# A trunk layer in float32 pieces: who splits the second output tile's weights, and when two late modulation steps run

## The chip, the cores and the metric

The kernel runs on one core of a Trainium2 chip. The metric is the time of one execution on the device in microseconds, taken as the median of several runs. The core has five engines with queues of their own: TensorE (PE, matrix products), VectorE (DVE), ScalarE (ACT), GpSimd (POOL) and SyncE (SP, which here issues all DMAs). They wait for each other through semaphores, counters that one engine raises and another waits on.

## The reference, cut to what matters

One layer of a diffusion backbone on 1024 tokens of width 1024, with a context of 256 tokens. The change lies around the output projection and the residual behind it, the last lines here:

```python
sh1, sc1, g1, sh2, sc2, g2 = [m[:, None, :] for m in adaln(c, w_mod[l], b_mod[l], N_MOD)]
h = modulate(x, norm1_w[l], sh1, sc1)
proj = h @ w_in[l]
...
# mix_and_mlp
mix = jnp.concatenate([y_gla, y_conv, y_pool], axis=-1) @ w_out
x = x + g1 * mix
h2 = modulate(x, norm2_w, sh2, sc2)
return x + g2 * (jnp.square(jax.nn.relu(h2 @ w_mlp1)) @ w_mlp2)
```

`adaln` is SiLU(c) times a 1024 x 6144 matrix; its six parts of 1024 columns are the shifts, scales and gates. The final RMSNorm follows. All in float32.

## The kernel before, in words

**Stages.** Tiles 0 to 19 of the weight stream are the input projection (`PROJ`), tiles 20 to 27 (`T_OUT` = 20, called output tiles 0 to 7 here) the output projection, then the first two tiles of the MLP, then the MLP with its own scheme of seven products in place of eight. In the input projection a tile is split by ScalarE (`weight_high`, L1411) and VectorE (`weight_low`, L1947). From output tile 0 on GpSimd does both passes (`split`, L766 and L769): a multiplication by ones for the high part, a subtraction for the low part.

**Around the change.** When the last input tile (CB1) is done, ScalarE rounds the six mixed blocks that were not ready earlier and VectorE subtracts (`low_mix(2)` to `low_mix(7)`); TensorE's output tile 0 takes the blocks in the same order and waits for each (`lo_made`). GpSimd, in queue order, splits output tile 0, output tile 1 (when CB1 is done and its slot so free), output tile 2 (when output tile 0 is done), and so on: `split_pairs`. TensorE waits at the start of each tile for `split_done`.

**The residual.** VectorE adds each finished output tile, times the gate, to `X` (`add`, L2189, which reads PSUM and frees one of TensorE's two accumulators), ScalarE squares the result and scales it (L1619, L1621), and VectorE adds the squares to `acc2` (L2192).

**Late modulation.** Two of the six parts of `adaln` (`sh2`, `g2`) are summed here by VectorE in 16 steps (`add_late(0)` to `add_late(15)`, L2173): a 128 x 1024 block of the matrix times a scalar, added to one of two sums. All operands lie in SBUF. The blocks, 512 KB each, come through four buffers: `load_late(i)` (L629) waits for step i - 4 from i = 4 on (`late_taken`). Before the change steps 0 to 3 stand ahead of the first addition to the residual, and two steps behind each of the six whole additions. TensorE needs the sums (`modulations_late`) in the last pair of output tiles.

**SP's queue** runs strictly in order: once all low parts are made (`lo_made`, 8) it issues `load_late(0)` to `(3)`, the second half of `X` (2 MB, L634), `load_late(4)` to `(7)`, then `load_tile(23)`, the weights of output tile 3; then for each further tile two late loads and the tile:

```python
sp.wait_ge(lo_made, KT)
for i in range(4):
    load_late(i)
sp.dma_start(X[:, 4:8, :], xt[4:8].rearrange("k p n -> p k n")).then_inc(x2_loaded[1], 16)
for i in range(4, 8):
    load_late(i)
load_tile(T_OUT + 3)
```

The order on each engine is the order in which the code is written; there is no planner in this part.

Of the kernel before, what the change touches and what calls it, by code (L numbers as in the profile page):

```python
# [19 lines left out]
ACT = mybir.ActivationFunctionType  # L20
# [32 lines left out]
T_OUT = NPROJ  # L53
# [146 lines left out]
def hybrid_trunk(nc, wstream, wg_in, wm1, wm2, xt, ct, small_in, gw_in, out):  # L200
    ctx = ExitStack()
    with ctx:
# [13 lines left out]
        raw = at("raw", [P, 2, KT, P], F32, raw_at)  # L216
        w_hi = at("w_hi", [P, 2, KT, P], F32R, w_hi_at)
# [156 lines left out]
        raw_loaded = [sem("raw_loaded0"), sem("raw_loaded1")]  # L374
# [6 lines left out]
        hi_made = sem("hi_made")  # L381
        split_done = sem("split_done")
        tile_done = sem("tile_done")
# [118 lines left out]
        def stream_free(t):  # L502

            return M_OF[PROJ[t]] + 1 if t < NPROJ else M_OUT + t - NPROJ + 1
# [248 lines left out]
        def _(pool):  # L753
# [10 lines left out]
            def split(b, n, linked):  # L764

                pool.tensor_tensor(w_hi[:, b, :, :], raw[:, b, :, :], ones.unsqueeze(1).broadcast_to([P, KT, P]),  # L766
                                   ALU.mult).then_inc(linked, 1)
                pool.wait_ge(linked, n)
                pool.tensor_tensor(w_lo[:, b, :, :], raw[:, b, :, :], w_hi[:, b, :, :].bitcast(F32),  # L769
                                   ALU.subtract).then_inc(split_done, 1)  # L770
# [17 lines left out]
            for t in range(NPROJ):  # L788
# [11 lines left out]
                if t >= 2 and PROJ[t - 2] in ("P0", "P1"):  # L800

                    i = int(PROJ[t - 2][1])
# [16 lines left out]
                        backward_states(h)  # L819
                        pool.wait_ge(states_backward, (NCH - 1) * (h + 1))  # L820
            pool.wait_ge(split_done, T_OUT)
            for t in (T_OUT, T_OUT + 1):
                pool.wait_ge(raw_loaded[t % 2], 16 * (t // 2 + 1))
                pool.wait_ge(tile_done, stream_free(t - 2))
                split(t % 2, t + 1, hi_made)
            def split_pairs(first, last):
                with pool.Fori(first, last) as i:
                    for b in range(2):
# [542 lines left out]
        def _(act):  # L1371
# [210 lines left out]
            for t, name in enumerate(PROJ):  # L1582
# [8 lines left out]
                m, i = M_OF[name], int(name[-1])  # L1591
# [9 lines left out]
            for n, k in enumerate(MIX_ORDER):  # L1601
# [8 lines left out]
                src, shape = mix_block(k)  # L1610
                act.activation(shape(mix_parts(k)[0]), src, ACT.Copy).then_inc(mix_hi, 1)  # L1611

            def residual_squares(m0, acc_made, sq_made, nth, sums_done, rs_made, between, after):

                def square(i, b):
                    act.wait_ge(main_free[1 - b], i + ((m0 + b) // 2 + 1))
                    act.wait_ge(acc_made, i * 2 + (b + 1))
                    xk = X[:, bass.ds(i * 2 + b, 1), :]
                    act.activation(sq2[:, :].unsqueeze(1), xk, ACT.Square).then_inc(sq_made, 1)  # L1619
                    if nth == 0:  # L1620
                        act.activation(xg[:, :, bass.ds(i * 2 + b, 1), :],  # L1621
                                       X[:, bass.ds(i * 2 + b, 1), :].rearrange("p k (h c) -> p h k c", h=2), ACT.Copy,
                                       scale=gain2[:, bass.ds(i * 2 + b, 1)]).then_inc(xg_made, 1)

                with act.Fori(0, KT // 2 - 1) as i:
                    for b in range(2):
                        square(i, b)

                def square_half(k, half, s_out):
                    cols = slice(half * HALF, (half + 1) * HALF)  # L1630
                    act.activation(sq2[:, cols], X[:, k, cols], ACT.Square).then_inc(s_out, 1)

                def scale_half(k, half):
                    if nth == 0:
                        cols = slice(half * HALF, (half + 1) * HALF)
                        act.activation(xg[:, half, k, :], X[:, k, cols], ACT.Copy, scale=gain2[:, k:k + 1]).then_inc(xg_made, 1)

                act.wait_ge(acc_made, KT - 1)
                act.wait_ge(res_half, 2 * nth + 1)
                square_half(KT - 2, 0, sq_made)  # L1640
                scale_half(KT - 2, 0)
                act.wait_ge(acc_made, KT)
                act.wait_ge(res_half, 2 * nth + 2)
                square_half(KT - 1, 0, sq_last)
                scale_half(KT - 1, 0)
                act.wait_ge(sums_done, 1)
                rsqrt(rs2[:, 0:HALF], sm[:, 0, :], D, rs_made)
                act.wait_ge(main_free[1], (m0 + KT - 2) // 2 + 1)
                square_half(KT - 2, 1, sq_made)
                scale_half(KT - 2, 1)  # L1650
                between()
                act.wait_ge(acc_made, KT + 1)
                act.wait_ge(main_free[0], (m0 + KT - 1) // 2 + 1)
                square_half(KT - 1, 1, sq_last)
                after()
                scale_half(KT - 1, 1)
                act.wait_ge(sums_done, 2)
                rsqrt(rs2[:, HALF:N], sm[:, 1, :], D, rs_made)
# [224 lines left out]
        def _(dve):  # L1883
# [61 lines left out]
            def weight_low(t):  # L1945
                dve.wait_ge(hi_made, t + 1)
                tt(w_lo[:, t % 2, :, :], raw[:, t % 2, :, :], w_hi[:, t % 2, :, :].bitcast(F32),  # L1947
                   ALU.subtract).then_inc(split_done, 1)
# [184 lines left out]
            def low_mix(n):  # L2133

                dve.wait_ge(mix_hi, n + 1)
                src, shape = mix_block(MIX_ORDER[n])
                hi, lo = mix_parts(MIX_ORDER[n])
                tt(shape(lo), src, shape(hi.bitcast(F32)), ALU.subtract).then_inc(lo_made, 1)  # L2138
# [3 lines left out]
            for t, name in enumerate(PROJ):  # L2142
# [8 lines left out]
                m, i = M_OF[name], int(name[-1])  # L2151
# [10 lines left out]

            for n in range(2, KT):
                low_mix(n)

            def add_late(i):

                dve.wait_ge(late_loaded[i % 4], 16 * (i // 4 + 1))
                if i < 2:
                    dve.wait_ge(late_cleared, 1)  # L2170
                else:
                    dve.wait_ge(late_taken, i - 1)
                stt(out=macc_late[:, i % 2, :], in0=mbuf_late[:, i % 4, :], scalar=silu_c[:, 2 * (i // 2):2 * (i // 2) + 1],  # L2173
                    in1=macc_late[:, i % 2, :], op0=ALU.mult, op1=ALU.add).then_inc(late_taken, 1)

            dve.wait_ge(o_done, 2 * HEADS)
            dve.memset(macc_late[:, :, :], 0.0).then_inc(late_cleared, 1)
            for i in range(4):
                add_late(i)

            def residual(m0, g, acc_made, sq_made, nth, between, after):

                dve.memset(acc2[:, :], 0.0).then_inc(acc_made, 1)
                dve.wait_ge(acc_made, 1)

                def add(i, b):
                    dve.wait_ge(tile_done, i * 2 + (m0 + b + 1))
                    xk = X[:, bass.ds(i * 2 + b, 1), :]
                    stt(out=xk, in0=main[:, 1 - b:2 - b, :], scalar=mods[:, g, bass.ds(i * 2 + b, 1)], in1=xk,  # L2189
                        op0=ALU.mult, op1=ALU.add).then_inc(main_free[1 - b], 1)  # L2190
                    dve.wait_ge(sq_made, i * 2 + (b + 1))
                    tt(acc2[:, :], acc2[:, :], sq2[:, :], ALU.add).then_inc(acc_made, 1)  # L2192
                    dve.wait_ge(acc_made, i * 2 + (b + 2))

                for i in range(KT // 2 - 1):
                    if i == 2:
                        dve.wait_ge(x2_loaded[1], 16)
                    for b in range(2):
                        add(i, b)
                        for n in range(2):  # L2200
                            add_late(4 + 4 * i + 2 * b + n)

                def add_half(k, half, s_out):
                    cols = slice(half * HALF, (half + 1) * HALF)
                    stt(out=X[:, k, cols], in0=main[:, (k + 1) % 2, cols], scalar=mods[:, g, k:k + 1], in1=X[:, k, cols],
                        op0=ALU.mult, op1=ALU.add).then_inc(s_out, 1)

                def sum_half(half):
                    cols = slice(half * HALF, (half + 1) * HALF)
                    dve.wait_ge(sq_made, KT - 1 + half)  # L2210
                    tt(acc2[:, cols], acc2[:, cols], sq2[:, cols], ALU.add).then_inc(acc_made, 1)

                dve.wait_ge(half_done, 2 * nth + 1)
                add_half(KT - 2, 0, res_half)
                sum_half(0)
                dve.wait_ge(half_done, 2 * nth + 2)
                add_half(KT - 1, 0, res_half)
                between()
                dve.wait_ge(tile_done, m0 + KT - 1)
                add_half(KT - 2, 1, main_free[1])  # L2220
                sum_half(1)
                after()
                dve.wait_ge(tile_done, m0 + KT)
                add_half(KT - 1, 1, main_free[0])
# [365 lines left out]
```

## Time and profile before

| what | value |
|---|---|
| median of 3 runs | 1144.76 us (1144.01 to 1144.79) |
| profiled execution | 1144.1 us |
| its span | 1142.3 us |
| TensorE matmul busy | 1093.3 us, 96% |
| VectorE busy | 833.2 us, 73% |
| ScalarE busy | 507.9 us, 44% |
| GpSimd busy | 336.1 us, 29% |
| mean granted clock of TensorE | 0.988 |

The profile records one execution. Times in it count from the start of its span, in microseconds; `L924` is a line of the kernel. A busy share is an average over stages with different limits. In a timeline, "[0.72 <-DVE X L2189]" behind an instruction says that its engine sat idle for 0.72 us before it, and that the last thing to arrive was VectorE's write of X at line 2189.

### The profile page before, as it was taken

How to read it: one execution, taken by the hardware profiler on the slowest of the kernel's cores; microseconds unless marked ns; L12 is line 12 of the kernel's file. 1: busy time of each engine (PE TensorE's matmuls, PEld its weight loads, DVE VectorE, ACT ScalarE, POOL GpSimd, SP SyncE). 2: the span in 40 equal slices, each digit the busy share in tenths (PEclk: the TensorE clock that was granted, in tenths of full speed). 3: DMA queues.
4: the chain of work that ended last, by engine and by line, in shares of the span. 5: the costliest groups of instructions: out<-in, count | busy, mean ns of one | idle time of the engine just before them, and what ended most of it. 6: DMA issues, size and time to landing. Idle time of an engine off the chain costs nothing.

```text
span 1142.3 us, 15381 instructions
## 1 busy us (share of the span) xinstructions
PE 1093.3 (96%) x5056; PEld 866.1 (76%) x5056; DVE 833.2 (73%) x1068; ACT 507.9 (44%) x823; POOL 336.1 (29%) x295
## 2 busy tenths in 40 slices
PE   8889999999999899887999999999899999999995
PEld 4468888877888688566888888888687877787783
DVE  3777869636444875799777777777977777687776
ACT  4556523355624222347666666666422122122234
POOL 1000006386202353522323233333322132123233
PEclk9899999999999999899999999999999999999998
DMA  9423241001013673204865757677827745955703
GB/s 370 195 93 100 88 144 38 25 32 38 20 37 129 239 237 132 74 9 155 329 263 225 267 222 264 222 270 272 336 96 273 278 186 198 331 211 187 263 1 147
DMA packets 58894, 199.71 MB, mean 175 GB/s; under 512 B 5600, under 2 KB 6880, under 8 KB 58336
## 3 DMA queue, kind: packets, MB, share of 16 engines
q1 hardware_dynamic: 58848, 199.11, 47.3%
q8 instruction: 28, 0.46, 0.2%
q14 instruction: 18, 0.15, 0.0%
HBM read 139.32 MB, written 59.77 MB: 174 GB/s over the span
## 4 chain that ended last, share of the span: by engine, by line
PE 45%; DMA 3%; DVE 2%; issue 1%; ACT 1%; SPq 0%; POOL 0%; DVEq 0%
PE main L1341 13%; PE ob L1300 13%; PE sm L1300 10%; PE sm L1341 5%; PE ob L1341 3%; DMA raw<-wstream 3%; DVE XR L2435 1%; DVE stage_last L2332 0%; SPq L662 0%; POOL XR L907 0%; DVE stage L2332 0%; DVE XR L2495 0%; ACT slot L1704 0%; DVE t_tmp L2325 0%; DVE hid L2345 0%
## 5 line engine op out<-in xcount | busy, mean ns | idle before, releaser
L1300 PE MATMUL ob<-h_sum,slot 128*128 128x512 f32 x540 | 133.3, 396 | 5.0 <-ACT hid L1747 3.1
L1704 ACT ACTIVATE slot<-raw 128x512 fp32r<-128x512 f32 x80 | 50.4, 631 | 181.0 <-PE main L1341 71.5
L924 PE MATMUL main<-a_hi,w_hi 128*128 128x512 f32 x376 | 125.9, 416 | 2.6 <-DVE a_lo L2138 2.6
L1300 PEld LDWEIGHTS ob<-h_sum,slot 128*128 128x128 f32 x540 | 102.3, 190 | 29.5 <-issue 3.9
L924 PE MATMUL main<-a_lo,w_hi 128*128 128x512 f32 x376 | 116.7, 392 | 0.0
L924 PE MATMUL main<-a_hi,w_lo 128*128 128x512 f32 x376 | 116.2, 390 | 0.0
L2435 DVE SCALAR_TENSOR_TENSOR XR<-main,mods,XR 128x512 f32<-128x512 f32 x112 | 82.8, 747 | 30.8 <-PE main L1341 29.1
L924 PEld LDWEIGHTS main<-a_hi,w_hi 128*128 128x128 f32 x376 | 66.7, 188 | 21.1 <-issue 5.8
L924 PEld LDWEIGHTS main<-a_hi,w_lo 128*128 128x128 f32 x376 | 70.6, 188 | 15.7
L924 PEld LDWEIGHTS main<-a_lo,w_hi 128*128 128x128 f32 x376 | 70.6, 188 | 15.6
L1300 PE MATMUL sm<-h_hi,slot 128*128 128x512 f32 x240 | 79.7, 393 | 0.6 <-ACT hid L1747 0.6
L2280 DVE TENSOR_TENSOR slot<-raw,slot 128x512 fp32r<-128x512 f32 x75 | 64.1, 855 | 21.7 <-ACT slot L1692 21.7
L1341 PE MATMUL main<-t_even,slot 128*128 128x512 f32 x336 | 79.3, 393 | 0.0
L782 POOL TENSOR_TENSOR scaled_state<-tst,decay 64x128 f32<-64x128 f32 x60 | 28.0, 467 | 162.6 <-ACT tst L1482 158.0
L1341 PEld LDWEIGHTS main<-t_even,slot 128*128 128x128 f32 x336 | 63.1, 188 | 14.2
L2285 DVE TENSOR_TENSOR slot<-raw,slot 128x512 fp32r<-128x512 f32 x80 | 57.6, 737 | 20.4 <-ACT slot L1704 20.4
L881 POOL TENSOR_TENSOR part_sum<-raw 128x512 f32<-128x512 f32 x16 | 21.3, 1333 | 137.8 <-DMA raw<-wstream 109.9
L766 POOL TENSOR_TENSOR w_hi<-raw,small 128x1024 fp32r<-128x1024 f32 x10 | 25.1, 2513 | 111.2 <-PE main L924 99.5
L865 POOL TENSOR_TENSOR held<-raw 128x512 f32<-128x512 f32 x15 | 24.9, 1657 | 111.5 <-DVE slot L2280 111.5
L1300 PEld LDWEIGHTS sm<-h_hi,slot 128*128 128x128 f32 x240 | 45.1, 188 | 11.0 <-issue 1.0
L1341 PE MATMUL main<-stage,slot 128*128 128x512 f32 x168 | 48.5, 397 | 3.6 <-DVE stage_last L2332 3.6
L2435 DVE SCALAR_TENSOR_TENSOR XR<-sm,mods,XR 128x512 f32<-128x512 f32 x64 | 46.5, 743 | 5.8 <-PE sm L1341 5.1
(334 smaller groups left out, 2508.7 us busy)
## 6 DMA issues: line engine op xcount, KB each, us to landing
hidden_kept<-stage SPq DMA_DIRECT2D x98, 512.0 KB, 4.3
raw<-wstream SPq DMA_DIRECT2D x60, 512.0 KB, 4.0
t_even<-hidden_kept SPq DMA_DIRECT2D x56, 512.0 KB, 4.6
raw<-wstream SPq DMA_DIRECT2D x16, 1024.0 KB, 7.9
stage<-hidden_kept SPq DMA_DIRECT2D x21, 512.0 KB, 3.7
stage_last<-hidden_kept SPq DMA_DIRECT2D x21, 512.0 KB, 4.6
wmod<-wm SPq DMA_DIRECT2D x4, 2048.0 KB, 23.4
mbuf<-wm SPq DMA_DIRECT2D x16, 512.0 KB, 3.9
```

What stands on the lines that cost most here:

```text
L766: pool.tensor_tensor(w_hi[:, b, :, :], raw[:, b, :, :], ones.unsqueeze(1).broadcast_to([P, KT, P]), ALU.mult).then_inc(linked, 1)
L782: pool.tensor_tensor(scaled_state[DK:P, :], tst[DK:P, h % 2, c, :], decay[DK:P, h, c:c + 1].broadcast_to([DK, DV]), ALU.mult).then_inc(sta ...
L865: pool.tensor_tensor(sums, a12, a11, ALU.subtract).then_inc(w1_sum, 1)
L881: pool.tensor_tensor(sums, a21, a22, ALU.add).then_inc(w2_sum, 1)
L924: ins = pe.matmul(main[:, bank, half * HALF:(half + 1) * HALF], w[:, slot, k, :], x[:, half * HALF:(half + 1) * HALF], start=begin, stop=end)
L1300: ins = pe.matmul(hid_bank(acc, odd), slots1[j][:, w, kp, :], parts[x][:, kp, :], start=PARTS[j][3] and kp == 0 and m == 0, stop=kp == KP ...
L1341: ins = pe.matmul(product_bank(s, acc, q), slots2[j][:, w, q, kp, :], tset[odd][j][kp][:, x, :], start=begins and kp == 0 and n == 0, stop ...
L1704: act.activation(slots2[j][:, 0, :, :, :], operand(s, j), ACT.Copy).then_inc(w2_hi, 1)
L2280: tt(slots1[j][:, 1, :, :], operand1(b, j), slots1[j][:, 0, :, :].bitcast(F32), ALU.subtract).then_inc(w1_lo, 1)
L2285: tt(slots2[j][:, 1, :, :, :], operand(s, j), slots2[j][:, 0, :, :, :].bitcast(F32), ALU.subtract).then_inc(w2_lo, 1)
L2435: stt(out=XR[m][:, cols], in0=product_bank(s, acc, q), scalar=mods[:, 3, m:m + 1], in1=XR[m][:, cols], op0=ALU.mult, op1=ALU.add).then_inc ...
```

## The change

Output tile 1's weights (stream tile `T_OUT + 1`) are no longer split by GpSimd: ScalarE writes the high part behind its last mix copy, VectorE the low part behind `low_mix(7)`. GpSimd waits for that split's end and goes on with the pairs from output tile 2. Late modulation steps 2 and 3 move from ahead of the first addition to the residual to behind it, so that four steps (2 to 5) follow that addition; the order of the steps among themselves, and the positions of steps 4 to 15, stay. SP's and TensorE's programs are unchanged.

```diff
--- before.py
+++ after.py
@@ -819,10 +819,10 @@
                         backward_states(h)
                         pool.wait_ge(states_backward, (NCH - 1) * (h + 1))
             pool.wait_ge(split_done, T_OUT)
-            for t in (T_OUT, T_OUT + 1):
-                pool.wait_ge(raw_loaded[t % 2], 16 * (t // 2 + 1))
-                pool.wait_ge(tile_done, stream_free(t - 2))
-                split(t % 2, t + 1, hi_made)
+            pool.wait_ge(raw_loaded[T_OUT % 2], 16 * (T_OUT // 2 + 1))
+            pool.wait_ge(tile_done, stream_free(T_OUT - 2))
+            split(T_OUT % 2, T_OUT + 1, hi_made)
+            pool.wait_ge(split_done, T_OUT + 2)
             def split_pairs(first, last):
                 with pool.Fori(first, last) as i:
                     for b in range(2):
@@ -1610,6 +1610,12 @@
                 src, shape = mix_block(k)
                 act.activation(shape(mix_parts(k)[0]), src, ACT.Copy).then_inc(mix_hi, 1)
 
+
+            act.wait_ge(split_done, T_OUT + 1)
+            act.wait_ge(raw_loaded[(T_OUT + 1) % 2], 16 * ((T_OUT + 1) // 2 + 1))
+            act.wait_ge(tile_done, stream_free(T_OUT - 1))
+            act.activation(w_hi[:, (T_OUT + 1) % 2, :, :], raw[:, (T_OUT + 1) % 2, :, :], ACT.Copy).then_inc(hi_made, 1)
+
             def residual_squares(m0, acc_made, sq_made, nth, sums_done, rs_made, between, after):
 
                 def square(i, b):
@@ -2162,6 +2168,7 @@
 
             for n in range(2, KT):
                 low_mix(n)
+            weight_low(T_OUT + 1)
 
             def add_late(i):
 
@@ -2175,8 +2182,8 @@
 
             dve.wait_ge(o_done, 2 * HEADS)
             dve.memset(macc_late[:, :, :], 0.0).then_inc(late_cleared, 1)
-            for i in range(4):
-                add_late(i)
+            add_late(0)
+            add_late(1)
 
             def residual(m0, g, acc_made, sq_made, nth, between, after):
 
@@ -2197,8 +2204,9 @@
                         dve.wait_ge(x2_loaded[1], 16)
                     for b in range(2):
                         add(i, b)
-                        for n in range(2):
-                            add_late(4 + 4 * i + 2 * b + n)
+                        at = 4 * i + 2 * b + (2 if (i, b) == (0, 0) else 4)
+                        for n in range(at, 8 + 4 * i + 2 * b - 2):
+                            add_late(n)
 
                 def add_half(k, half, s_out):
                     cols = slice(half * HALF, (half + 1) * HALF)
```

## Rows read from the trace of the kernel before

**Rows 1.** TensorE's timeline (start us, length us): starts of output tiles 0 to 4.
```profile
369.71 0.63 PE L924 MATMUL main<-early_hi,w_hi 128*128 128x512 f32 x2
...
376.90 0.74 PE L924 MATMUL main<-a_hi,w_hi 128*128 128x512 f32 x2 [1.67 <-DVE a_lo L2138]
...
383.88 0.63 PE L924 MATMUL main<-early_hi,w_hi 128*128 128x512 f32 x2
...
395.77 0.73 PE L924 MATMUL main<-early_hi,w_hi 128*128 128x512 f32 x2 [0.72 <-DVE X L2189]
...
406.88 0.40 PE L924 MATMUL main<-early_hi,w_hi 128*128 128x512 f32 x1
...
417.89 0.63 PE L924 MATMUL main<-early_hi,w_hi 128*128 128x512 f32 x2
```

**Rows 2.** Timeline of GpSimd (POOL): splits of output tiles 1 to 4.
```profile
370.02 2.41 POOL L766 TENSOR_TENSOR w_hi<-raw,small 128x1024 fp32r<-128x1024 f32 x1 [5.96 <-PE main L924]
...
372.51 3.26 POOL L769 TENSOR_TENSOR w_lo<-raw,w_hi 128x1024 fp32r<-128x1024 f32 x1
...
384.12 2.40 POOL L766 TENSOR_TENSOR w_hi<-raw,small 128x1024 fp32r<-128x1024 f32 x1 [8.36 <-PE main L924]
...
400.57 2.47 POOL L766 TENSOR_TENSOR w_hi<-raw,small 128x1024 fp32r<-128x1024 f32 x1 [10.72 <-DMA raw<-wstream]
...
403.12 2.40 POOL L769 TENSOR_TENSOR w_lo<-raw,w_hi 128x1024 fp32r<-128x1024 f32 x1
...
407.12 3.06 POOL L766 TENSOR_TENSOR w_hi<-raw,small 128x1024 fp32r<-128x1024 f32 x1 [1.60 <-PE main L924]
```

**Rows 3.** Timeline of VectorE (DVE): low parts, late steps, first addition and its sum.
```profile
371.05 2.46 DVE L2138 TENSOR_TENSOR a_lo<-ypool,a_hi 128x1024 fp32r<-128x1024 f32 x1
...
373.44 3.41 DVE L2138 TENSOR_TENSOR a_lo<-ypool,a_hi 128x1024 fp32r<-128x1024 f32 x1
...
376.77 1.21 DVE L2138 TENSOR_TENSOR a_lo<-yconv,a_hi 128x1024 fp32r<-128x1024 f32 x1
...
381.76 1.76 DVE L2177 MEMSET macc_late<- 128x2048 f32 x1 [0.38 <-issue]
...
384.69 2.90 DVE L2173 SCALAR_TENSOR_TENSOR macc_late<-mbuf_late,silu_c,macc_late 128x1024 f32<-128x1024 f32 x1 [1.16 <-DMA mbuf_late<-wm]
...
387.52 3.41 DVE L2173 SCALAR_TENSOR_TENSOR macc_late<-mbuf_late,silu_c,macc_late 128x1024 f32<-128x1024 f32 x1
...
393.49 0.91 DVE L2183 MEMSET acc<- 128x1024 f32 x1 [0.16 <-issue]
...
394.43 1.28 DVE L2189 SCALAR_TENSOR_TENSOR X<-main,mods,X 128x1024 f32<-128x1024 f32 x1
...
397.02 1.23 DVE L2192 TENSOR_TENSOR acc<-acc,sq 128x1024 f32<-128x1024 f32 x1 [1.31 <-ACT sq L1619]
...
398.28 2.48 DVE L2173 SCALAR_TENSOR_TENSOR macc_late<-mbuf_late,silu_c,macc_late 128x1024 f32<-128x1024 f32 x2
```

**Rows 4.** ScalarE's and VectorE's timeline: an earlier split; end of ScalarE's pause.
```profile
351.36 1.04 ACT L1411 ACTIVATE w_hi<-raw 128x1024 fp32r<-128x1024 f32 x1
...
352.44 1.23 DVE L1947 TENSOR_TENSOR w_lo<-raw,w_hi 128x1024 fp32r<-128x1024 f32 x1 [9.26 <-ACT w_hi L1411]
...
395.93 1.06 ACT L1619 ACTIVATE sq<-X 128x1024 f32 x1 [20.22 <-DVE X L2189]
```

**Rows 5.** SP: issue of tile 3's weights; landings of weights issued at 401.2, 411.7.
```profile
393.72 0.43 SPq L595 DMA_DIRECT2D raw<-wstream  x1
...
DMA to landing us min/median/max: 5.2/5.2/5.2
...
DMA to landing us min/median/max: 4.3/4.3/4.3
```

**Rows 6.** TensorE behind a stall: timeline, windows (granted clock third from last).
```profile
472.58 0.62 PE L1265 MATMUL main<-h_hi,w_hi 128*128 128x512 f32 x1 [3.44 <-DVE h_lo L2241]
...
476.00:478.00 2.00, 2.00 (x5) 1.48 (x6) 2.00 (x4) 0.00 (x0) 0.00 (x0) 0.50 0.00 0
```

## The prediction

> **What bounds the kernel now.** The matrix engine is busy nearly throughout, so a change beside it is worth only what it takes off a wait of that engine, and only if the next wait does not give it back. I read its timeline over the first output tiles first [rows 1]. A clean output tile takes 11.01 us (406.88 to 417.89). Tile 0 takes 383.88 - 369.71 = 14.17 us, 3.16 too many, and the row at 376.90 names who ended one of its two stalls: VectorE's low parts of the mixed activations (L2138). Tile 1 takes 395.77 - 383.88 = 11.89, 0.88 too many, ended by VectorE's first addition to the residual (L2189). Tile 2 takes 11.11: its first pair of matmuls after a stall is some 0.1 slow. So 3.16 + 0.88 + 0.10 = 4.14 us is all that this stage can return; tiles 3 to 5 run without a gap.
>
> Then GpSimd's and VectorE's timelines, side by side [rows 2, 3]. A low part takes 1.21 us with nothing on GpSimd (376.77) and one follows the other 1.14 later. The two at 371.05 and 373.44 take 2.46 and 3.41. The first ends at 373.51, 1.08 after GpSimd's split instruction of 370.02 (ended 372.43); the second ends at 376.85, 1.08 after the one of 372.51 (ended 375.77, 3.26 long for the usual 2.41; 2.26 of it behind VectorE's end at 373.51). So GpSimd and a VectorE instruction with both inputs in SBUF take turns: whoever started second waits for the whole of the other. An addition that reads PSUM doesn't wait (394.43: 1.28).
>
> **Part 1: the split of output tile 1's weights leaves GpSimd.** GpSimd's two instructions (2.41 + 3.26) go. ScalarE gets one copy, 1.04 us (at 351.36) [rows 4], right behind its last mix copy near 375.7: it has nothing else until 395.93, an idle time of 20.22, so it costs nothing there. VectorE gets one subtraction, 1.23 (at 352.44) [rows 4], behind the six low parts. These now run unblocked: six by 1.14 from 371.05 end at 377.94, where before they ended at 381.38 (0.38 ahead of the memset at 381.76 [rows 3]): 3.44 earlier. Low part 2 ends at 372.27 and is needed at 372.5, low part 3 at 373.4 against 373.9, and later ones have more: I take the whole 3.16 as gone (bounds 2.9 to 3.16, for a slow pair of 0.1 or two). Tile 1 starts on the matrix engine at 380.72. Its low weights are ready at 377.9 + 1.2 = 379.1, 1.6 to spare. GpSimd's added wait for both halves of tile 1 (ahead of its split of tile 2) is over at 379.1 too, before the end of tile 0 for which it waits anyway; nothing on ScalarE is queued behind its three added waits until the first square near 390.
>
> **What this moves.** The loads of modulation steps 0 to 3 wait for the last low part, so step 0 can start at 384.69 - 3.44 = 381.25; the added subtraction, 0.38 of issue and the memset (1.76) end at 381.2, just under it. GpSimd starts splitting tile 2 when tile 0 ends: 384.12 - 3.16 = 380.96, again first by 0.3 us. Then the old pattern repeats: from GpSimd's start (384.12) to the end of step 1 (387.52 + 3.41) it was 6.81 us; now step 1 ends at 387.8.
>
> **Part 2: steps 2 and 3 behind the first addition.** Before, they stood ahead of it. Now the accumulator's memset (0.16 + 0.91) follows step 1, the addition runs from 388.9 to 390.2, and the matrix engine needs its bank at 380.72 + 11.01 = 391.73. The stall of 0.88 and its slow pair go. Left in place, the two steps (2.4 us) would have kept the addition to 392.6 and the stall alive, about as long as before. Tile 2 now starts at 391.73 and ends at 402.74: 4.14 us gained at this point. The moved steps cost VectorE nothing in all, but each also releases a DMA: SP issues load 6 after step 2 and load 7 after step 3, and output tile 3's weights stand in SP's queue behind load 7. Before, step 3 ended at 393.33 (0.16 ahead of the memset at 393.49) and the weights were issued at 393.72, 0.4 later. Now step 3 comes after the first addition's sum: the sum starts 397.02 - 394.43 = 2.59 after the addition, at 391.5, the first of the steps 1.26 behind it, and the second has ended 398.28 + 2.48 - 397.02 = 3.74 behind it: at 395.2. **The weights of tile 3 are issued at 395.6, 1.9 us later than before**, while the matrix engine wants them split 4.14 earlier.
>
> **Does the transfer make it up?** Before, it was in a full queue and GpSimd waited for it until 400.57 (10.72 idle, ended by the DMA [rows 2]); the split ended at 403.12 + 2.40 = 405.52, with 1.36 to spare. Now everything else is landed by then except loads 6 and 7. Two rows bound it [rows 5]: the weights issued at 411.7, right behind one late load, landed in 4.3 us; those issued at 401.2, behind two late loads 1.2 apart as here, in 5.2. So it lands at 399.9 to 400.8, and GpSimd starts within 0.15, at 400.1 to 401.0: about where it started before. Steps 2 to 5 end on VectorE at 391.5 + 1.26 + 4 x 1.2 = 397.6, the second addition follows, and its sum (both inputs in SBUF) starts 2.59 later, at 400.16. If GpSimd is first (a landing by 400.0), its high part takes 2.47, the low part waits for the sum (3.26), split done at 405.9. If the sum is first, GpSimd waits until 401.4 (so came the 3.06 of the high part at 407.12), takes 2.26, waits for step 6 (1.08) and takes 2.26 again: 407.0. The middle landing, 400.4, and the nearer row, 5.2, both give the second. So tile 3 starts on the matrix engine at 407.1 with a slow pair of 0.1, that is 407.2 against 406.88: **all of the 4.14 is given back and 0.3 us more.** The bounds: 404.9 for the split (landing 399.9, nobody in the way: 4.95) to 407.9 (landing 400.8 plus 0.15, 4.95 and two waits of 1.1).
>
> Behind it nothing new is late: tile 4's weights are issued with steps 4 and 5 near 398, split right after tile 3's by 413, needed at 418; from there additions, steps and splits follow the matrix engine's tiles as before. The profiled execution took 1144.10 around a span of 1142.3; 0.3 more is 1144.4. The runs' median, 1144.76, lies 0.66 above that execution, so on the runs' scale I say **1145.1 us**.
>
> The Trainium skill (SBUF — State Buffer, "The DMA setup-cost knee") puts a transfer at about 2 us plus its bytes at 436 GB/s. By it the 512 KB weights would take 3.2 alone and, behind load 7, 4.0; the landing would be 399.7, GpSimd would be ahead of the sum, and the kernel would gain about 1 us. The row with the like spacing, 5.2, says otherwise, and my sum goes by the row.
>
> **The rivals.**
> (a) GpSimd gets in front of the sum: the landing is by 400.0, the split is done at 404.9 to 405.9, tile 3 starts 0.8 to 1.8 earlier than before: 1143.0 to 1144.0. For it: the 4.3 row. Against it: the 5.2 row.
> (b) VectorE wins the earlier turn, step 0 (381.25) before GpSimd's high part (380.96). Then step 0 ends at 382.5, step 1 at 385.9, all of VectorE is 1.9 earlier, the weights are issued at 393.7, and the split is done 1.9 earlier than in the forecast or in (a): 1.6 to 2.8 gained, near 1142.6. Against it: 0.3 us of lead for GpSimd; three rows [rows 2, 3] show who starts first, wins. For it: both starts come from unlike chains.
> (c) The weights of tile 3 are in time after all (a landing by 397.5, for instance because the emptied queue is faster than any row here): the whole 4.14 stays, 1140.6. Against it: the shortest landing behind a late load is 4.3.
> (d) The change gives nothing of what it says: the two slow low parts weren't GpSimd's doing, and all stays near 1144.8. The two ends 1.08 behind GpSimd's speak against it.
> (e) The other side, slower: the matrix engine's clock falls. Its two stalls of this stage become one, from 403.0 to 407.1, 4.1 us idle. After the idle time of 3.44 that ended at 472.58 the granted clock was at 0.50, 1.2 GHz [rows 6]: 5 matmuls in 2 us, where a clean tile's 48 in 11.01 make 8.7. Each us at the lower level thus costs some 0.43, and 3 to 5 us of it 1.3 to 2.1. With the 0.3 that is 1146.4 to 1147.2. It decides, as slower, once the engine stays low for more than 4.7 us or the weights land after 401. Against it: behind the shorter stalls of 1.67 and 0.72 [rows 1] the matrix engine went on at full speed (tile 2 took 11.11), and nothing here shows from what length on it doesn't.
>
> The Trainium skill (TensorE: Matmul & The Clock Gate, "What's actually happening") says that idle time brings the clock down to 1.2 GHz and busy time brings it back; rows 6 agree with it, and it would favour (e).
>
> **How the numbers follow.** Forecast 0.42 (own range 1144.5 to 1145.8), (a) 0.18, (b) 0.10, (c) 0.08, (d) 0.04, (e) 0.18. About 0.2%, 2.3 us, can't be told from no change: faster means under 1142.5, slower over 1147.0. Faster: (c) whole, half of (b), a little of (a): 0.15. Slower: a third of (e): 0.06. The rest, 0.79, is no change. The range runs from 1141.4, which leaves out (c), to 1147.0.
>
> **What would show it.** Right: the low parts all near 1.2 us; tile 1 starting at 380.7 and tile 2 at 391.7 without a stall; the load of tile 3's weights issued near 395.6; a stall of the matrix engine near 403 to 407, ended by GpSimd's low part. Wrong: that issue at 393.7 or earlier, no stall ahead of tile 3 (then (b) or (c)), or a granted clock of 0.5 behind it (then (e)).

## The result, and the profile after

The changed kernel took 1148.62 us, the median of 7 runs (1145.35 to 1150.15), against 1144.79 before (7 runs, 1144.01 to 1146.26): ratio 1.0027, 95% interval 1.0014 to 1.0040. It is slower by some 3 us: the two medians lie 3.8 apart, and the ratio, which later sections use for differences, stands for 3.1 (1.6 to 4.6). The forecast was 1145.1 in a range of 1141.4 to 1147.0.

The profiled execution took 1145.35 us around a span of 1143.6: it was the quickest of the seven and stands only 1.3 above the one of before. Its tile 0 starts 1.0 us earlier than before's, for reasons ahead of the change, so times of after are to be read with 1.0 added, or as differences. TensorE's timeline after (start, length; the starts of output tiles 0 to 4), to be set against [rows 1]:

```profile
368.71 0.63 PE L924 MATMUL main<-early_hi,w_hi 128*128 128x512 f32 x2
...
379.72 0.63 PE L924 MATMUL main<-early_hi,w_hi 128*128 128x512 f32 x2
...
390.74 0.63 PE L924 MATMUL main<-early_hi,w_hi 128*128 128x512 f32 x2
...
407.28 1.22 PE L924 MATMUL main<-early_hi,w_hi 128*128 128x512 f32 x2 [5.37 <-POOL w_lo L769]
...
419.64 0.63 PE L924 MATMUL main<-early_hi,w_hi 128*128 128x512 f32 x2
```

Tiles 0 and 1 now take 11.01 and 11.02 us: 3.16 and 0.87 are gone. Then TensorE stands still for 5.37 us ahead of tile 3, and tile 3 itself takes 12.36 in place of 11.01. From tile 0 to tile 4 it is 50.93 us, against 48.18 before: 2.75 more. VectorE's timeline after, against [rows 3]:

```profile
370.05 2.35 DVE L2144 TENSOR_TENSOR a_lo<-ypool,a_hi 128x1024 fp32r<-128x1024 f32 x2
...
376.86 1.22 DVE L1953 TENSOR_TENSOR w_lo<-raw,w_hi 128x1024 fp32r<-128x1024 f32 x1
378.45 1.76 DVE L2184 MEMSET macc_late<- 128x2048 f32 x1 [0.38 <-issue]
380.32 6.46 DVE L2180 SCALAR_TENSOR_TENSOR macc_late<-mbuf_late,silu_c,macc_late 128x1024 f32<-128x1024 f32 x2
386.94 0.91 DVE L2190 MEMSET acc<- 128x1024 f32 x1 [0.16 <-issue]
387.89 1.29 DVE L2196 SCALAR_TENSOR_TENSOR X<-main,mods,X 128x1024 f32<-128x1024 f32 x1
390.48 1.22 DVE L2199 TENSOR_TENSOR acc<-acc,sq 128x1024 f32<-128x1024 f32 x1 [1.30 <-ACT sq L1625]
391.74 4.87 DVE L2180 SCALAR_TENSOR_TENSOR macc_late<-mbuf_late,silu_c,macc_late 128x1024 f32<-128x1024 f32 x4
396.53 1.28 DVE L2196 SCALAR_TENSOR_TENSOR X<-main,mods,X 128x1024 f32<-128x1024 f32 x1
399.11 1.22 DVE L2199 TENSOR_TENSOR acc<-acc,sq 128x1024 f32<-128x1024 f32 x1 [1.30 <-ACT sq L1625]
400.37 4.58 DVE L2180 SCALAR_TENSOR_TENSOR macc_late<-mbuf_late,silu_c,macc_late 128x1024 f32<-128x1024 f32 x2
```

With 1.0 added, the first addition starts at 388.9 and the second sum at 400.1, both to 0.1 us where the prediction put them. GpSimd's timeline after (the splits of tiles 2 and 3), against [rows 2], shows what came after:

```profile
379.97 2.39 POOL L766 TENSOR_TENSOR w_hi<-raw,small 128x1024 fp32r<-128x1024 f32 x1 [16.91 <-PE main L924]
382.44 3.26 POOL L769 TENSOR_TENSOR w_lo<-raw,w_hi 128x1024 fp32r<-128x1024 f32 x1
401.31 2.56 POOL L766 TENSOR_TENSOR w_hi<-raw,small 128x1024 fp32r<-128x1024 f32 x1 [15.61 <-DMA raw<-wstream]
403.94 3.21 POOL L769 TENSOR_TENSOR w_lo<-raw,w_hi 128x1024 fp32r<-128x1024 f32 x1
```

GpSimd waits 15.61 us for tile 3's weights. SP's timeline has their issue at 394.62, 1.0 added 395.6, again as predicted, and the answer for that one transfer says when they were there, 6.5 us later [rows 5]:

```profile
394.25 0.33 SPq L629 DMA_DIRECT2D mbuf_late<-wm  x1
394.62 0.43 SPq L595 DMA_DIRECT2D raw<-wstream  x1
...
DMA to landing us min/median/max: 6.5/6.5/6.5
```

The windows view of after (stretch, busy times; the granted clock is the third number from the end, and (x6) behind TensorE's busy time counts its matmuls) shows the rest, TensorE's standstill and what its clock did behind it [rows 6]:

```profile
402.00:406.00 4.00, 0.00 (x0) 0.00 (x0) 4.00 (x2) 0.00 (x0) 3.92 (x2) 1.00 0.81 313
407.00:410.00 3.00, 2.72 (x6) 2.15 (x7) 2.56 (x1) 1.45 (x2) 2.92 (x3) 0.50 0.74 258
```

### The profile page after: what moved, and what is told of

The parts are those of the page before. It is cut to its first block, busy times and chain, and to the rows that moved or that the text cites. A ratio compares the mean times of both kernels' runs of the same rounds, so it can differ in the third digit from the quotient of the medians.

```text
span 1143.6 us, 15381 instructions
## 1 busy us (share of the span) xinstructions
PE 1092.1 (96%) x5056; PEld 865.4 (76%) x5056; DVE 833.2 (73%) x1069; ACT 508.8 (44%) x824; POOL 330.8 (29%) x293
## 4 chain that ended last, share of the span: by engine, by line
PE 44%; DMA 4%; DVE 2%; issue 1%; ACT 1%; SPq 0%; POOL 0%; DVEq 0%; ACTq 0%
PE main L1341 13%; PE ob L1300 13%; PE sm L1300 10%; PE sm L1341 5%; DMA raw<-wstream 3%; PE ob L1341 3%; DMA hidden_kept<-stage 1%; DVE XR L2443 1%; DVE stage_last L2340 0%; DVE stage L2340 0%; SPq L662 0%; POOL XR L907 0%; DVE XR L2503 0%; ACT slot L1710 0%; DVE t_tmp L2333 0%
## 5 line engine op out<-in xcount | busy, mean ns | idle before, releaser
L766 POOL TENSOR_TENSOR w_hi<-raw,small 128x1024 fp32r<-128x1024 f32 x9 | 22.2, 2466 | 119.5 <-PE main L924 102.9
```

## The experiments

My theory after the result was the chain of the prediction with larger ends: step 3 comes later, so do tile 3's weights, TensorE waits, and its clock falls. Its rivals: the handover of the split to ScalarE and VectorE costs it; or nothing was lost but luck with the clock.

**The changed kernel again**, without an edit.

> The changed kernel, run again beside the others. Theory 1 (the weights of output tile 3 are issued behind late loads 6 and 7, land late, TensorE stands still for over 4 us ahead of tile 3 and its clock falls behind that): 1147 to 1150 us, a stall of 4.5 to 6 us ended by GpSimd's low part, granted clock 0.5 right behind it. Rival 2 (the handover of the split to ScalarE and VectorE costs it, through VectorE's longer queue): the same time, so this run doesn't tell the two apart. Rival 3 (the seven runs were unlucky in where the clock fell, not slower by the stall): within 0.2% of the kernel before, 1143 to 1147, with clock levels that differ from the last profile.

1147.93 us (12 runs, 1144.08 to 1150.30), ratio 1.0029 (1.0015 to 1.0042). This time the profiled execution was one of the slower ones (1148.89, span 1147.1). The stall is the same to the hundredth, the clock stays low for longer:

```profile
408.47 1.22 PE L924 MATMUL main<-early_hi,w_hi 128*128 128x512 f32 x2 [5.37 <-POOL w_lo L769]
```
```profile
410.00:414.00 4.00, 4.00 (x14) 3.19 (x13) 3.96 (x2) 0.00 (x0) 3.92 (x2) 0.70 0.27 102
```

Tile 0 to tile 4 is 421.32 - 369.90 = 51.42, 3.24 more than before. With the same stall in a second profile and an interval above 1 in a second set of runs, luck as the whole cause is out.

**Part 1 alone**: steps 2 and 3 back ahead of the first addition.

```diff
-            add_late(0)
-            add_late(1)
+            for i in range(4):
+                add_late(i)
...
-                        at = 4 * i + 2 * b + (2 if (i, b) == (0, 0) else 4)
-                        for n in range(at, 8 + 4 * i + 2 * b - 2):
-                            add_late(n)
+                        for n in range(2):
+                            add_late(4 + 4 * i + 2 * b + n)
```

> The handover of tile 1's split alone; steps 2 and 3 stay ahead of the first addition. Theory 1: the weights of tile 3 are issued near 390.6 on the scale of the kernel before (3 us earlier than there), land near 397 to 398, are split by 404 or so; the 3.16 us in tile 0 are gone, the stall of 0.9 ahead of tile 2 stays or grows by 0.5: 1141.5 to 1143, no stall over 1.5 us ahead of tile 3. Rival 2 (the handover costs it): 1147 to 1150, as with both parts.

1141.34 us (12 runs), ratio 0.9975 (0.9965 to 0.9985): 2.9 us faster than before. TensorE has a single stall from tile 0 to tile 4, the old one, and GpSimd starts on tile 3's weights 28.1 us behind the start of tile 0, where it was 31.8 and 32.6 in the changed kernel:

```profile
391.17 0.73 PE L924 MATMUL main<-early_hi,w_hi 128*128 128x512 f32 x2 [0.72 <-DVE X L2196]
```
```profile
396.37 2.41 POOL L766 TENSOR_TENSOR w_hi<-raw,small 128x1024 fp32r<-128x1024 f32 x1 [11.12 <-DMA raw<-wstream]
```

The handover isn't the cost, it is the gain: from tile 0 to tile 4 it is 413.37 - 368.27 = 45.10 us, 3.08 less than before. The stall of 0.72 that part 2 was meant to remove stays.

**Part 2 alone**: the kernel before with only the moved steps (the last two hunks of the change).

> The two late steps moved alone; GpSimd splits tile 1 as before. Theory 1: tile 0 keeps its 14.2 us, the stall ahead of tile 2 (0.72) goes, step 3 ends near 398.3 and the weights of tile 3 are issued near 398.7, 5 us later than before; they land at 403 to 405, are split by 408.5 to 411, and TensorE needs them at 406: a stall of 3 to 5 us ahead of tile 3, 1146.5 to 1149. Rival 2 (the handover costs it): no stall ahead of tile 3 and 1144, as before or 0.9 less.

1150.77 us (6 runs), ratio 1.0050 (1.0032 to 1.0068). The standstill of 4.09 us and the slow pair (1.22) are there without the handover; I had expected up to 1149:

```profile
408.77 1.22 PE L924 MATMUL main<-early_hi,w_hi 128*128 128x512 f32 x2 [4.09 <-POOL w_lo L769]
```

So the moved steps make the loss, by 5.7 us here. The tile starts agree: tile 0 to tile 4 is 422.08 - 368.35 = 53.73 us, 5.55 more than before. Tile 3 alone took 422.08 - 408.77 = 13.31 in place of 11.01, more than in the changed kernel, though the stall ahead of it was shorter.

**Tile 3's weights ahead of late loads 6 and 7**, in the changed kernel.

```diff
-            for i in range(4, 8):
+            for i in range(4, 6):
                 load_late(i)
             load_tile(T_OUT + 3)
+            for i in range(6, 8):
+                load_late(i)
```

> The changed kernel with one thing more: SP issues the weights of tile 3 ahead of late loads 6 and 7 (behind load 5), so they no longer wait for steps 2 and 3. Theory 1: issued near 388 on the scale of the kernel before, landed by 396, split by 401.5, ahead of TensorE's need at 402.7; no stall between tile 0 and tile 5; the whole 4.1 us stays: 1140 to 1141.5. Rival 2 (the handover): still 1147 to 1150. Rival 3 (clock luck): the scatter of the changed kernel stays, whatever the stall does.

1140.59 us (9 runs, 1137.43 to 1141.32), ratio 0.9962 (0.9950 to 0.9975). With the steps where the change put them and only SP's order mended, the loss of 3.3 turns into a gain of 4.3. The weights are issued 386.70 - 368.24 = 18.46 us behind the start of tile 0 (25.91 in the changed kernel), and GpSimd starts on them long before TensorE needs them:

```profile
386.70 0.43 SPq L595 DMA_DIRECT2D raw<-wstream  x1
```
```profile
393.02 2.98 POOL L768 TENSOR_TENSOR w_hi<-raw,small 128x1024 fp32r<-128x1024 f32 x1 [7.80 <-DMA raw<-wstream]
```

Tile 0 to tile 4 takes 412.77 - 368.24 = 44.53 us. The only stall left is a new one, of 0.24. The second addition stands behind steps 2 to 5, and these now run beside GpSimd's split of tile 3 and take 9.16 us in place of 4.87:

```profile
401.67 0.73 PE L926 MATMUL main<-early_hi,w_hi 128*128 128x512 f32 x2 [0.24 <-DVE X L2198]
```

**The same mend in the kernel before**, and **part 1 alone with it** (the same diff).

> The kernel before with only SP's order changed: tile 3's weights ahead of late loads 6 and 7. Theory 1: it had no stall ahead of tile 3, so it moves by less than 0.5 us, 1144 to 1145. Rival (the new order of the loads is what pays in tile_first, by itself): 1141 or so.

> Part 1 alone (steps 0 to 3 ahead of the first addition) and the weights of tile 3 issued ahead of late loads 6 and 7. Theory 1: as tile_first, but with the stall of 0.7 to 0.9 ahead of tile 2, so 0.8 to 1 us above it: 1141.3 to 1141.8, the same as part 1 alone (there the weights came in time anyway). Rival (the moved steps are what pays once the weights are in time, or they cost something of their own): off from that by more than 1 us.

1144.02 us, ratio 0.9997 (0.9988 to 1.0006), and 1140.43 us (8 runs), ratio 0.9972 (0.9960 to 0.9985). The mend shows no gain where the weights weren't late. And part 2 is worth little once they are in time: from tile 0 to tile 4 it is 45.02 us without the moved steps and 44.53 with them; the 0.5 us can't be told in the times. (I had expected 1141.3 to 1141.8 for part 1 with the mend; it came 0.9 lower.)

**The stall filled**: 16 spare matmuls ahead of the wait for tile 3's weights; their result isn't read.

```diff
+                    if b == 1:
+                        for _ in range(fill):
+                            pe.matmul(sm[:, 0, :], a_hi[:, 2, 0:P], a_hi[:, 2, 0:HALF], start=True, stop=True)
...
-            with pe.Fori(1, KT // 2 - 1) as i:
-                out_pair(i + ((M_OUT - 2) // 2 + 1), i * 2 + (T_OUT + 1), False)
+            for i in range(1, KT // 2 - 1):
+                out_pair(i + ((M_OUT - 2) // 2 + 1), i * 2 + (T_OUT + 1), False, fill=16 if i == 1 else 0)
```

> The changed kernel with 16 spare matmuls (128x512, 0.23 us each, 3.7 us, into a bank that nothing reads) on TensorE ahead of its wait for tile 3's weights; the loop over the two middle pairs is written out for it. The stall itself, 5.4 us from the end of tile 2 to tile 3, stays. Theory 1 with the clock's fall as a cost of its own: granted clock 1.00 behind the stall, and 1.5 to 3 us less than the changed kernel: 1145 to 1146.5, that is 0.5 to 1.5 over the kernel before (5.4 of stall less 4.14 taken away). Rival (the clock's fall costs nothing that shows, the whole loss is the wait): 1148, as the changed kernel.

1145.65 us (11 runs), ratio 1.0015 (1.0006 to 1.0023), where the changed kernel had 1.0029: 1.6 us less with 3.8 us of useless work added. The two intervals overlap, so the size is better read from the tile starts: tile 0 to tile 4 is 418.29 - 368.63 = 49.66 us, 1.27 and 1.76 less than in the two profiles of the changed kernel, and tile 3 takes 11.11. GpSimd's split ends no earlier, but the granted clock stays at 1.00:

```profile
401.66 3.79 PE L1217 MATMUL sm<-a_hi 128*128 128x512 f32 x16
...
407.18 0.73 PE L924 MATMUL main<-early_hi,w_hi 128*128 128x512 f32 x2 [1.73 <-POOL w_lo L769]
```
```profile
407.00:410.00 3.00, 2.82 (x12) 2.32 (x13) 2.59 (x1) 1.42 (x2) 2.92 (x3) 1.00 0.64 234
```

12 matmuls in 3 us in place of 6. So the clock's fall is about half of the changed kernel's loss (1.27 of 2.75, 1.76 of 3.24); the rest is the wait beyond what was gained. (The loop is also written out in this kernel; what that does by itself wasn't measured.)

**The loads kept apart**: SP waits for tile 3's weights before it issues anything behind them.

```diff
             load_tile(T_OUT + 3)
+            sp.wait_ge(raw_loaded[(T_OUT + 3) % 2], 16 * ((T_OUT + 3) // 2 + 1))
```

> The changed kernel in which SP waits, behind the issue of tile 3's weights, until they have landed, before it issues late loads 8 and 9 and tile 4's weights. If the transfers issued behind them share the bandwidth, tile 3's weights land in 4.3 to 5.0 us in place of 5.8 to 6.5, and the stall is 1 us shorter: 1146 to 1147.5. If transfers are served in the order of issue, they land in 5.8 to 6.5 as before and the time is 1148 or more.

1148.49 us (10 runs), ratio 1.0034 (1.0021 to 1.0047). The time is that of the second expectation, the changed kernel's. The transfer took 5.6 us, against 6.5 and 5.8 in the two profiles of the changed kernel: between the two expectations, so whether later transfers share the bandwidth stays open. Part 2 alone, where late loads and tile 4's weights do follow, had 5.4, so they are at least not all of it. But the run showed something else. Counted from the start of tile 0 (at 369.00 here), GpSimd starts on the weights at 31.71 us, against 32.60 and 31.84 in the two profiles of the changed kernel, and is done at 38.45, against 38.44 and 38.43; the stall is 5.37 once more:

```profile
400.71 3.45 POOL L767 TENSOR_TENSOR w_hi<-raw,small 128x1024 fp32r<-128x1024 f32 x1 [14.72 <-DMA raw<-wstream]
404.24 3.21 POOL L770 TENSOR_TENSOR w_lo<-raw,w_hi 128x1024 fp32r<-128x1024 f32 x1
...
407.58 1.22 PE L925 MATMUL main<-early_hi,w_hi 128*128 128x512 f32 x2 [5.37 <-POOL w_lo L770]
```

**VectorE out of the way**: steps 6 and 7 behind the third addition in place of the second.

```diff
-                        at = 4 * i + 2 * b + (2 if (i, b) == (0, 0) else 4)
-                        for n in range(at, 8 + 4 * i + 2 * b - 2):
+                        steps = {(0, 0): range(2, 6), (0, 1): (), (1, 0): range(6, 10)}
+                        for n in steps.get((i, b), range(4 + 4 * i + 2 * b, 6 + 4 * i + 2 * b)):
                             add_late(n)
```

> The changed kernel with late steps 6 and 7 moved once more, from behind the second addition to behind the third (there with steps 8 and 9), so VectorE is idle while GpSimd splits tile 3's weights. The stall ahead of tile 3 was 5.37 us in three runs though the weights landed in 5.6 to 6.5 us. Theory 1a (the turns that GpSimd and VectorE take round the split set its end, the landing only picks the turn): GpSimd's two instructions take 2.4 us each, without a wait, the stall shrinks from 5.37 to 4.2 to 4.5, and the time to 1146.5 to 1147.5. Rival (the landing alone sets it): 5.4 again.

1147.13 us (7 runs), ratio 1.0025 (1.0014 to 1.0036), which can't be told from the changed kernel's 1.0029. The weights were as late (6.4 us), GpSimd's instructions take 2.37 and 2.35, and the stall is 1.2 shorter:

```profile
400.95 2.37 POOL L766 TENSOR_TENSOR w_hi<-raw,small 128x1024 fp32r<-128x1024 f32 x1 [15.45 <-DMA raw<-wstream]
403.40 2.35 POOL L769 TENSOR_TENSOR w_lo<-raw,w_hi 128x1024 fp32r<-128x1024 f32 x1
```
```profile
405.88 0.73 PE L924 MATMUL main<-early_hi,w_hi 128*128 128x512 f32 x2 [4.16 <-POOL w_lo L769]
```

The first pair of tile 3 runs at full speed here, and still the clock falls, a little later (0.50 from 408 to 410):

```profile
406.00:410.00 4.00, 4.00 (x11) 3.13 (x12) 3.96 (x2) 0.00 (x0) 3.92 (x2) 0.57 0.01 4
```

Tile 3 took 418.53 - 405.88 = 12.65 us, and tile 0 to tile 4 is 50.00.

**A version meant to keep it all**: the mend for tile 3, each further tile's weights ahead of the two late loads beside it, and steps 2 to 4 behind the first addition, 5 to 7 behind the second.

```diff
+                load_tile(t)
                 for i in range(2 * (t - T_OUT), min(2 * (t - T_OUT) + 2, NLATE)):
                     load_late(i)
-                load_tile(t)
...
+                        steps = {(0, 0): range(2, 5), (0, 1): range(5, 8)}
```

> A version meant to keep all of it: part 1; steps 0, 1 ahead of the first addition, 2 to 4 behind it, 5 to 7 behind the second, the rest as they were; and SP issues each output tile's weights ahead of the two late loads beside it, tile 3's ahead of late loads 6 and 7. Theory 1: no stall from tile 0 to tile 6, also not the 0.24 ahead of tile 3 that tile_first has; 0.3 us less than tile_first, which is within its noise: 1139.8 to 1141. Rival (late loads that now wait for splits stop VectorE's steps): a stall ended by VectorE ahead of a tile from 4 on, or in the last pair, and over 1141.5.

1139.60 us (7 runs, 1138.21 to 1144.10), ratio 0.9964 (0.9952 to 0.9977): TensorE has no wait at all in the output projection's first six tiles in its profile, and the time is that of the simpler mend within its interval. The profiled execution was the slowest of the seven (1144.10), so what made it slow lies outside these tiles. Both versions beat the kernel before and the changed one.

## Why the prediction was wrong

**Right, to 0.1 or 0.2 us:** the low parts unblocked (six in 6.9), tile 1 at 11.0 behind tile 0, the stall ahead of tile 2 gone, GpSimd first in the turn around tile 2's split, the issue of tile 3's weights 1.9 later than before, the second sum at 400.1. Right too was that all of the 4.14 is given back by those weights, and that the gains of this stage can be priced by TensorE's tile starts: 3.08 us for part 1 alone by the tiles, 2.9 by the times; for part 2 alone 5.55 more by the tiles, 5.7 by the times.

**The step that failed is "Does the transfer make it up?"**, whose landing came out too early by 0.6 to 1.3 us, together with the clock's fall, which the sum put at nothing and left to rival (e). By the tile starts the stage was forecast 0.3 us longer than before and measured 2.75 and 3.24 longer. Tile 3 started 1.1 later than forecast in both profiles, and then took 1.35 and 1.84 longer than a clean tile: 0.3 + 1.1 + 1.35 = 2.75 and 0.3 + 1.1 + 1.84 = 3.24.

First, the landing. I had 4.3 to 5.2 us from two rows of before [rows 5]; it was 6.5 and 5.8 in the two profiles of the changed kernel, 6.5 with the stall filled, 5.6 with the loads apart, 6.4 with VectorE out of the way and 5.4 with part 2 alone. I took the queue to be empty but for loads 6 and 7. It was, from 392 to 394; but late loads 6 and 7 and the weights, issued within 1.6 us of each other, were moved at 291 and 236 GB/s in the windows from 394 to 398, where the queue had run at 424 before. My two rows were also kinder than the case: in before, nothing was issued behind the weights of 401.2 until 407.94, nor behind those of 411.7 until 416.34, while in the changed kernel two late loads and tile 4's weights followed within 2.4 us. Why the transfers are slow wasn't settled.

Second, the turn. The later landing put GpSimd not behind the sum but behind step 6, one VectorE instruction on, and its low part behind step 7. These are steps 6 and 7 and the third addition in the profile of after:

```profile
400.37 1.28 DVE L2180 SCALAR_TENSOR_TENSOR macc_late<-mbuf_late,silu_c,macc_late 128x1024 f32<-128x1024 f32 x1
...
401.57 3.38 DVE L2180 SCALAR_TENSOR_TENSOR macc_late<-mbuf_late,silu_c,macc_late 128x1024 f32<-128x1024 f32 x1
404.87 1.27 DVE L2196 SCALAR_TENSOR_TENSOR X<-main,mods,X 128x1024 f32<-128x1024 f32 x1
```

The split was done at 403.94 + 3.21 = 407.15, with 1.0 added 408.15, against a forecast of 407.0. The stall of 5.37 in three profiles whose GpSimd starts lie up to 0.9 us apart, and 4.16 with VectorE idle, show that the turn sets the end, and the landing only picks the turn. The bound of 407.9 was added up wrongly: its own terms, 400.8 + 0.15 + 4.95 + 2 x 1.1, make 408.1. That this lies so near the measured 408.15 is luck, since the landing was later than its 400.8 and the waits were shorter than two of 1.1. The rule of the turns that I had read off [rows 2, 3] was the right one, but one of its readings was not: no instruction of GpSimd ran beside the addition at 394.43, so that row doesn't show that an addition reading PSUM goes unblocked. The row at 404.87 above does, 1.27 us beside GpSimd's low part of 403.94.

Third, the clock. Rival (e) was the right one, in both of its conditions: the clock fell, and the weights landed after 401 (at 402.1 and 401.4 on the scale of before). I gave it 0.18 since nothing showed from which idle time on the clock falls; yet the row behind 3.44 us idle [rows 6] lay under my own forecast of 4.1, and only stalls of 1.67 and less spoke against it. Each profile with a standstill of 4.09 us or more and no filling has the low clock behind it. The price was as in (e), 1.35 and 1.84 us for tile 3 (12.36 and 12.85 us in place of 11.01); over all five such profiles it was 1.35 to 2.30, and the shortest stall, 4.09, had the highest. Had I put the likely case at (e), 1146.4 to 1147.2, the landing and the turn, 1.1 us, would still have been missing.

## What to carry to other kernels

A step that is moved moves every transfer that waits for it, and everything issued behind that transfer on the same queue: look there first, and put the load that the bottleneck needs ahead of the ones that only a side chain needs. Two instructions earlier or later in such a queue were worth 7 us between the changed kernel and its mend, more than the change itself. Where a stall is forecast longer than one behind which the trace shows the low clock, the low clock belongs in the forecast, not among the rivals.

## What the runs showed of the hardware that was not expected

GpSimd's and VectorE's turns round waits up: in three profiles starts spread over 0.9 us gave the same end of the split to 0.02 us. The Trainium skill (SBUF — State Buffer, "Who interferes with whom") says that of a GpSimd instruction and a VectorE instruction with two inputs in SBUF the one that issues first holds the shared ports to its end. These traces agree: step 7 beside GpSimd's high part took 3.38 us in place of 1.2, and the addition that reads PSUM took 1.27 beside the low part.

What the low clock costs behind one and the same stall differs: in the three profiles with a stall of 5.37 (the changed kernel twice, then the loads kept apart) tile 3 took 12.36, 12.85 and 12.48 us.

Where TensorE's clock is low later in the kernel differs from profile to profile as well. In the window 454 to 460 the granted clock was 0.72 before and 1.00 after:

```profile
454.00:460.00 6.00, 6.00 (x20) 3.88 (x20) 0.17 (x1) 0.00 (x0) 0.00 (x0) 0.72 0.01 3
```
```profile
454.00:460.00 6.00, 6.00 (x36) 4.76 (x35) 0.33 (x2) 1.02 (x2) 0.00 (x0) 1.00 0.01 3
```

The counts of matmuls in these windows can't be compared, since the kernel after is 1.75 us behind here and most of its 16 more are small ones of the late modulation. The same instructions can: from the first of these small matmuls (L1232) to the first matmul of the next stage (L1265) it was 472.58 - 450.99 = 21.59 us before, 472.73 - 452.74 = 19.99 after, and 477.57 - 454.42 = 23.15 in the changed kernel run again. So the profiled execution after got 1.6 us back there and the other lost 1.56 more, which goes some way to say why the first was the best of its seven; it wasn't tested by itself. The same program scattered over 5 us (1141.98 to 1147.54 before, 26 runs in one session), so three runs of each might not have shown the sign of this change.
